# Value products of the neighbourhood heads: one query tile at a time instead of half by half

## What is computed

```python
def _neighbourhood_attention(q, k, v, rpb):
    ...
    for cb in range(GRID_W // NA_QCB):
        ...
        s = jnp.einsum('brqhe,brkche->brhqkc', qblk, kblk).astype(jnp.float32) * (Dh ** -0.5)
        s = jnp.where(colmask[:, None, :], s + bias, NEG_INF)
        p = jax.nn.softmax(s, axis=(-2, -1))
        outs.append(jnp.einsum('brhqkc,brkche->brqhe', p.astype(v.dtype), vblk))
    return jnp.concatenate(outs, axis=2).reshape(B, S, H, Dh)
```

## Time and profile before

| what | us |
|---|---|
| device time, median of 3 runs | 2051.58 (2051.21 to 2051.70) |
| device time of the profiled execution | 2053.82 |
| its span | 2052.0 |
| phase of the neighbourhood heads in it, scores of unit 1 to the last copy out | 1087.8 to 1284.6 |

### The profile page before, as it was taken

One profiled execution on the slowest core, in us unless ns is written; L12 is line 12 of the kernel. 1 busy time (PEld: TensorE's weight loads), 2 busy tenths in 40 slices (PEclk: granted clock), 3 DMA queues, 4 the chain that ended last, 5 costly groups with the idle time before them and its releaser, 6 DMA issues. The chain is left out here.

```text
span 2052.0 us, 27549 instructions
## 1 busy us (share of the span) xinstructions
PE 1939.4 (95%) x10090; PEld 1537.8 (75%) x10090; DVE 1195.6 (58%) x2036; ACT 834.6 (41%) x1459; POOL 606.5 (30%) x431
## 2 busy tenths in 40 slices
PE   6899999999999969999889997889999999999997
PEld 4677777777878857767568885777788888888786
DVE  5865545555676963344535555587744444457878
ACT  4533333333434663333424555336433333334443
POOL 0253443332970000000024331001543443439500
PEclk9999999999999989999999999999999999999999
DMA  9165455454875323111032220612233233258733
GB/s 322 59 201 164 160 173 177 154 171 164 319 248 161 111 65 101 32 52 41 11 85 52 62 62 32 236 72 93 88 123 103 88 118 103 93 204 288 261 109 118
DMA packets 184886, 270.58 MB, mean 132 GB/s; under 512 B 12592, under 2 KB 111152, under 8 KB 184624
## 3 DMA queue, kind: packets, MB, share of 16 engines
q1 hardware_dynamic: 153888, 235.18, 34.1%
q10 hardware_dynamic: 29840, 29.50, 4.5%
q0 software_dynamic: 1024, 4.13, 1.2%
HBM read 210.84 MB, written 57.93 MB: 131 GB/s over the span
## 5 line engine op out<-in xcount | busy, mean ns | idle before, releaser
L1624 PE MATMUL f_ps<-f_uh,f_ops 128*128 128x512 f32 x2496 | 782.1, 392 | 13.3 <-ACT acc L1049 4.5
L1624 PEld LDWEIGHTS f_ps<-f_uh,f_ops 128*128 128x128 f32 x2496 | 469.2, 188 | 127.6 <-issue 23.9
L1624 PE MATMUL f_ps<-f_ul,f_ops 128*128 128x512 f32 x1248 | 487.0, 390 | 0.0
L969 POOL TENSOR_TENSOR f_sums<-f_raw 128x512 f32<-128x512 f32 x80 | 113.5, 1418 | 548.4 <-DVE f_ul L1422 242.3
L1624 PEld LDWEIGHTS f_ps<-f_ul,f_ops 128*128 128x128 f32 x1248 | 234.8, 188 | 47.2
L1452 DVE TENSOR_TENSOR f_dl<-f_blocks,f_dh 128x1024 fp32r<-128x1024 f32 (+1 forms) x146 | 201.3, 1393 | 81.9 <-ACT f_dh L1165 81.7
L1165 ACT CAST f_dh<-f_blocks 128x1024 fp32r<-128x1024 f32 (+1 forms) x146 | 144.3, 990 | 222.7 <-PE f_ps L1758 217.2
L1293 DVE TENSOR_TENSOR f_ops<-f_sums,f_ops 128x512 fp32r<-128x512 f32 x160 | 120.7, 756 | 139.8 <-ACT f_ops L1030 139.7
L1758 PE MATMUL f_ps<-f_dh 128*128 128x512 f32 x496 | 194.2, 391 | 5.0 <-DVE f_dl L1452 4.2
L1758 PE MATMUL f_ps<-f_dl,f_dh 128*128 128x512 f32 x496 | 193.6, 390 | 0.0
L1758 PE MATMUL f_ps<-f_dh,f_dl 128*128 128x512 f32 x496 | 193.5, 390 | 0.0
(11 more groups left out here) (262 smaller groups left out, 3028.9 us busy)
## 6 DMA issues: line engine op xcount, KB each, us to landing
f_hidden<-acc SPq DMA_DIRECT2D x154, 256.0 KB, 3.8
f_blocks<-f_hidden SPq DMA_DIRECT2D x154, 256.0 KB, 3.5
f_blocks<-in_ffn_w_down SPq DMA_DIRECT2D x132, 256.0 KB, 5.9
f_raw<-in_ffn_w_gate SPq DMA_DIRECT2D x20, 1024.0 KB, 6.1
f_raw<-in_ffn_w_up SPq DMA_DIRECT2D x20, 1024.0 KB, 5.4
f_aw<-in_w_ada ACTq DMA_DIRECT2D x28, 512.0 KB, 3.6
acc<-in_w_ada ACTq DMA_DIRECT2D x28, 512.0 KB, 4.7
in_raw<-in_w_in SPq DMA_DIRECT2D x24, 512.0 KB, 3.9
```

What stands on the lines that cost most here:

```text
L969: nc.gpsimd.tensor_tensor(sums[:, x], of, with_, how).then_inc(s_done, 1)
L1624: done = nc.tensor.matmul(ps[:, bank, :], l[:, k, :], r[:, k, :], start=fresh and k == 0 and m == 0, stop=closed and k == HK - 1 and m == ...
```

## The change

For the neighbourhood heads, the 24 matmuls of a half are cut into four *parts* of six, one for each query tile (two heads by three key tiles), in the same order of sums. `parts_due` puts the first half's parts in steps 8, 9, 10 and 11 of a pair, and the second half's in steps 13, 15, 17 and 19. Each part waits only for the ACT copies of its own query tile's two units and those before. `pv` now counts parts, and `turned_out` waits ahead of every second unit for the part of the half before that read the same place in `pt`. The dilated heads keep their order (one part for each half).

```diff
+    def parts_due(s):
+
+        if dil:
+            return [] if half_due(s) is None else [(half_due(s), 0)]
+        u = s - LAG - 1
+        p, m = u // NU, u % NU
+        if u >= 0 and CBS <= m < UN:
+            return [(HALVES * p, m - CBS)]
+        if u >= 0 and m >= UN and m % 2:
+            return [(HALVES * p + 1, (m - UN) // 2)]
+        return []
+
+    PARTS = 1 if dil else CBS
...
-                if n == 0 and h >= 1:
-                    act.wait_ge(pv, h)
+                if h >= 1 and (n % 2 == 0 if PARTS > 1 else n == 0):
+                    act.wait_ge(pv, PARTS * (h - 1) + n * PARTS // UN + 1)
...
-                    dve.wait_ge(pv, HALVES * p)
+                    dve.wait_ge(pv, PARTS * HALVES * p)
...
-                dve.wait_ge(pv, h + 1)
+                dve.wait_ge(pv, PARTS * (h + 1))
...
-            def multiply(h):
+            def multiply(h, part):
                 p, half = h // HALVES, h % HALVES
-                pe.wait_ge(p_out, UN * (h + 1))
-                if half == 0:
+                todo = list(enumerate(products(dil, half)))
+                each = len(todo) // PARTS
+                pe.wait_ge(p_out, UN * h + UN * (part + 1) // PARTS)
+                if half == 0 and part == 0:
                     pe.wait_ge(v_out, NVG * (p + 1))
-                if p >= 1:
+                if p >= 1 and part == 0:
                     pe.wait_ge(y_out, HALVES * (p - 1) + half + 1)
-                todo = products(dil, half)
-                for n, (x, users, cls) in enumerate(todo):
+                for n, (x, users, cls) in todo[each * part:each * part + each]:
...
-                if half_due(s) is not None:
-                    multiply(half_due(s))
+                for h, part in parts_due(s):
+                    multiply(h, part)
```

## The result

| | before | changed |
|---|---|---|
| device time, median of 20 runs (us) | 2051.61 | 2055.57 |
| ratio changed / before, 95% interval | | 1.0015 (1.0009 to 1.0022) |
| profiled execution: device time, span (us) | 2053.82, 2052.0 | 2053.34, 2051.5 |

A forecast was written before the change was run, and what follows sets the result against it. PE's own instructions bound pairs 0 to 2; the way from a score over DVE and ACT back to PE bounds pair 3. Terms +2.1, -1.9 and -1.5 gave -1.3 us: 2050.3 us from 2051.58, range 2045.5 to 2055.5.

The forecast's parts named there:

- ACT's 16.9 us: ACT's five waits behind the bursts of `mix_o`, where PE is full: removing them counted at nothing.
- the three waits at the changes of pairs: PE's waits for the next queries' low parts, 1.01, 1.01 and 0.71 us, filled by parts: -2.7 us.
- the free step 8 of pairs 1 and 2: First part there needs the last value tiles; nine projections ahead leave 0.5 us of cover: cost 0.
- the gain of step 51: Pair 3: six instructions instead of a burst follow the ACT copy, -1.9 us with the clock equal.
- the price of a lot: Pairs 0 to 2, up to unit 48: 17 more lots at 0.20 us each for opening and closing, +3.4 us.
- the clock: Pair 3: half the 3.0 us cost of PE's lower clock goes, -1.5 us; bounds -3.0 and +3.
- 24 records moved forward: Two parts of the sixth half move from behind unit 48 to before it: +1.4 us there.
- Rival C: Lots cost 0.4 us each through wait and signal: +3.4 before unit 48, about +1 in pair 3; 2054.7 us, chance 0.13.
- The rule of the Trainium skill: Small idle times between matmul groups let the clock fall repeatedly, so spread parts would not keep it up.
- rival D: Clock low through most of pair 3: +10 us, 2061.8 us, chance 0.05.
- steps 56 to 59: Pair 3: first part waits for the value copy, last burst shrinks; +0.3, -0.6 us carried forward and taken.
- Steps 60 to the end: Pair 3: parts delay scores and transposes, last burst shrinks; together +0.6 us, bounds -2.1 and +1.4.

The follow-up runs named there:

- double_lots: Changed kernel with the second to fourth parts of halves 0 to 4 each cut in two, 15 more lots; 2060.30 us, ratio to before 1.0037.
- side_by_side: Changed kernel with each half's four parts, own waits and signals kept, one behind the other where the burst stood before; 2048.93 us, ratio to before 0.9980.
- fill_two: side_by_side with 24 records of the second half of pairs 0 and 1 moved as one lot into the pair's last step; 2048.21 us, ratio to before 0.9982.
- fill_waits: side_by_side with 24-record lots moved to the last step of pairs 0 and 1, half 5 in steps 47, 49 and 51; 2048.03 us.
- bursts_0_4: Changed kernel with halves 0 to 4 back to bursts, halves 5 to 7 still in parts; 2050.98 us, ratio to before 0.9996.
- behind_turns: Changed kernel with parts of halves 0 to 4 one step later, between transposes and projections; 2055.59 us, ratio to before 1.0017.
- full_width: Changed kernel with 128 instead of 64 weight columns per value product in halves 0 to 4, not computing the layer; 2062.47 us in one run.
- bursts_5_7: Changed kernel with halves 5 to 7 back to bursts, halves 0 to 4 still in parts; 2054.92 us, ratio to before 1.0014.
- first_part_late: Changed kernel with the first part of half 6 in step 57 instead of step 56; 2052.55 us, ratio to before 1.0006.
- side_again: The kernel of side_by_side measured once more, on the chip of later runs; 2047.62 us, ratio to before 0.9984.

## Why the forecast was wrong

Right were the way of reading (PE's own instructions count in pairs 0 to 2, waits in pair 3), that ACT's 16.9 us bring nothing, that the three waits at the changes of pairs fill up, the free step 8 of pairs 1 and 2, and the gain of step 51 (units 48 to 52 take 10.88 us instead of 13.19, about 0.7 of it by less low clock). Two terms failed, and their errors add up: the price of a lot, and the clock.

**The lot, first term of part 1.** Forecast 17 x 0.20 = +3.4 us, from the two visible edges. What was missing is the constant inside the lot, which I had spread over the burst's 48 records by dividing. Counted from start to start over all of PE's records between unit 4 and unit 48, before and changed, a lot costs 0.09 us at its opening, 0.15 inside and 0.11 at the score behind it: 0.35 us, near the 0.36 of double_lots. The terms:

| | us |
|---|---|
| openings, 17 x 0.09 | +1.6 |
| inside, 17 x 0.15 | +2.6 |
| closings, 14 x 0.11 | +1.5 |
| 24 records moved forward | +1.3 |
| the three waits | -3.2 |
| sum; measured | +3.7; +3.70 |

Three closings don't count: two scores behind a wait had theirs before, too, and the third lies behind unit 48. So the lots cost 5.6 us instead of 3.4. The waits gave back more than the forecast's 2.7: the idle times of the earlier trace rows count from the end of the last projection, while from its start to the score's it was 1.41, 1.41 and 1.11 us where 0.23 is the ordinary distance. The 0.31 us a lot of the expectations, with waits at 2.7, came near M1 because these two errors partly cancel.

The bound I gave for a lot, 0.40, held; the number taken was too low. Rival C had the size nearly right, but its reason, a wait and a signal for each part, is refuted by side_by_side. Its time of 2054.7 us is what the ratio gives (2051.6 + 3.1), by other terms than its own: that is luck.

**The clock.** Forecast -1.5 us, half of the cost gone. In the profile the lower clock did not shrink but grew, from 10.2 to 13.7 us, and cost about 0.8 us more instead. The price of a us at the lower clock can be read where no kernel of this study has a part or a burst, from unit 52 to unit 56: 9.50 us without low clock (fill_two), 9.83 to 9.89 with 0.9 to 1.6 us of it, 10.69 to 10.85 with 3.9 or 4.0, 11.11 and 11.14 with 7.2 and 7.3, 11.64 with 8.2 (fill_waits): 0.2 to 0.4 us for each us of it. Five profiles with the parts of halves 5 to 7 placed as changed (the changed kernel, bursts_0_4, behind_turns, full_width, double_lots) have 13.7, 13.7, 13.7, 13.7 and 6.8 us of low clock in M2, and M2 of 43.95, 44.37, 43.64, 43.65 and 42.41: again some 0.2 us for each, though one profile stands against four. The two with plain bursts there (before, bursts_5_7) have 10.2 us and 44.21 and 44.20.

The rule of the Trainium skill named in the forecast ("TensorE: Matmul & The Clock Gate", "A second HAM failure mode: psum-queue depth-cycling") pointed that way. The trace agrees weakly: four of the five have more low clock than before, one less, and first_part_late, with all parts as well, has 10.2 us. The mean granted clock of whole executions doesn't settle it. It is 0.9826 in 20 runs of the changed kernel and 0.9838 in 83 of before, but bursts_5_7, with no part in pair 3, has 0.9827 beside 0.9832 for the runs of before in its set, and bursts_0_4, with parts there, 0.9837. It was far from rival D's size. Why it should be more is argued from order only, the burst of step 51 during which the clock came back before being gone; with stretches that move by themselves from one execution to the next, no run here isolates it.

**Pair 3, stretch by stretch.** The time at the lower clock stands in brackets; the last column takes 0.22 us off for each us of it.

| units | before | changed | forecast, clock equal | measured, clock equal (estimate) |
|---|---|---|---|---|
| 48 to 52 | 13.19 (6.8) | 10.88 (3.4) | -1.9 | -1.6 |
| 52 to 56 | 9.84 (1.3) | 10.85 (4.0) | no term | +0.4 |
| 56 to 60 | 10.20 (2.1) | 10.39 (6.2) | -0.6 | -0.7 |
| 60 to the copy out | 10.98 (0) | 11.83 (0) | +0.6 | +0.9 |

So at equal clock the parts save about 1.0 us of pair 3, where the forecast had 1.9, and the longer low clock takes 0.8 of them back.

For steps 56 to 59 I set two numbers beside each other, +0.3 and -0.6 carried forward, and took the carried one. The raw difference, +0.2, seems to speak for the hand sum, but four more us of it lay at the lower clock; double_lots, with the same order there, has 9.82 us with 3.4 of low clock, less than before's 10.20 with 2.1. The carried number was about right. The wait inside it is real: first_part_late shows it at about 1.4 us (1.6 by hand), and it could have been had as a gain.

Steps 60 to the end came to 11.83 against 10.98 us, +0.85, forecast +0.6 and bound +1.4: the scores of unit 62 start 3.52 us behind those of unit 61 instead of 1.28, more than the 1.7 us of delay that I allowed for step 61; the next unit takes 0.76 of it back, and the end 0.64.

The sum by its measured terms is +3.7 - 0.3 = +3.4 us, and the ratio says +3.1.

## What to carry over

Where an engine is full, moving work earlier can only fill its waits, and cutting it into pieces costs an edge for each: price the edge from a lot as short as the one planned, or record by record at both ends of a long one, never by dividing a long one. A consumer's long wait for a burst is no prize while the burst is being computed by the bottleneck. What did pay was to leave the order alone and let the burst start when its first inputs are there: waits cut finely, matmuls kept together.

## What was not expected of the hardware

- Matmuls with 64 columns of weights behind ones with 128 begin with a late weight load: 0.32 us instead of 0.23 to the first record, and 0.15 us once for a lot beyond 0.055 us a record, most of it between the last records and the next full-width matmul (0.20 us); with 128 columns the opening is gone and the way out takes 0.03 us (full_width). Twelve such records cost 1.25 us with full-width weights and 0.80 with half-width ones.
- Waits and signals within a run of matmuls cost nothing measurable when they are already satisfied: 48 records take 2.77 us with one of each or with four.
- The time of one program varies by about 2 us (standard deviation over the runs of before) together with its mean granted clock; over these runs a us at the lower clock goes with 0.2 us more. Two orders that differ by 1.7 us in a full stretch (side_again, fill_two) could not be told apart by eleven runs each.
